# A hybrid attention and MoE layer on one core: where the transposes of x stand, and the scheme of the first q round

## Chip, core and metric

The kernel runs on one core of a Trainium2 chip. The metric is the device time of one execution in microseconds (us). Everything is float32. One core has the matrix engine PE (TensorE; its weight loads are listed apart as PEld), the vector engine DVE (VectorE), the activation engine ACT (ScalarE), POOL (GpSimd), and SP (SyncE), whose queue issues most DMAs. Each engine works through its instructions in order and waits on semaphores. PE writes to psum only, 8 banks of 512 float32 columns on 128 partitions.

## What is computed

One layer over 512 latent and 128 context tokens (640 rows of 1024). Cut to what bears on the change:

```python
mod = silu(c) @ w_ada + b_ada                 # 2 vectors (latent, context), 6 x 1024 columns each
shift1, scale1, gate1, shift2, scale2, gate2 = split(mod, 6)
h = rms_norm(x, norm1_g) * (1 + scale1) + shift1
z = h @ w_in                                  # cb, cc, cx, q, k, v, gc, ga
q = rms_norm(q.reshape(b, l, 8, 2, 64), q_norm_g)      # the same for k
if latent: q, k = axial_rope(q), axial_rope(k)
s = softmax(q k / sqrt(64)) of both halves;  a = p[0] - lam * p[1];  o = rms_norm(a @ v)
lam = exp(sum(lambda_q1 * lambda_k1)) - exp(sum(lambda_q2 * lambda_k2)) + lam_init
mixed = sigmoid(gc) * y_conv + sigmoid(ga) * (o @ w_attn_out)
x = x + gate1 * (mixed @ w_o)
x = x + gate2 * hier_moe(rms_norm(x, norm2_g) * (1 + scale2) + shift2)   # 16 experts, top 2 of a group
```

## The kernel before

The order of every engine's work is written out by hand; there is no planner. The stages are: load x and the first modulation weights; modulation and transposed h (`hT`, 8 blocks of 128 features by 640 tokens); for each of two groups of four heads a q round, a k round, a v round and attention; then feature products, the output projection, routing, and the 16 experts.

**Start.** The modulation is `silu(c) @ w_ada`, made in pairs of two 512-column pieces, pair p by the job `ada` p: 8 k-steps times 2 lanes, each a 64-row by 512-column matmul. In the records one float32 matmul is two, so a job has 32. The row result is copied from psum by ACT (`ada_copy`, L774), transposed by PE (job `adaT`, L1677), and DVE adds the bias and makes the scale (L1063, L1070). Pairs 0 and 1 are shift1 and scale1, half of the features each. Their weights stand in the four slots of `weight_ring` and come in two halves (`s_early`, then `s_w`). PE also transposes the normalized x (`xn`): the job `xT` k is feature block k, 5 transposes into two psum banks. ACT (odd k, L785) or DVE (even k, L1079) then writes `hT` block k as scale times psum plus shift, so it needs the modulation of that block's pair: pair 0 for k under 4, pair 1 for the others. With two banks each, only four jobs of the start fit in psum.

**Rounds.** A round makes q, k or v of one group of heads: 640 tokens by 512 columns. There are two schemes:

- plain: five tiles of 128 tokens (`tok_job`), each 8 matmuls of 512 columns; tile 0 (`i == 0`) stands apart in two halves of 64 tokens and has 16.
- seven products (`product_mm`): tile 0 is made plainly, and the other four tiles in two sets of seven products p1 to p7 (Strassen's scheme, 4 matmuls of 256 columns each), 14 products in all. It needs four sums of `hT` (`th`, by DVE, `token_sums`, held in the memory of x) and four sums of the weights (`round_sum`, by POOL, L622). DVE reads the products out and adds them up (`read_product`, L1151 and L1164), ACT copies p1 (`first_copy`). They leave rows in `v_sb`, `kept`.

Before the change the very first q round (m = 0) was plain, all other rounds used products. After each tile: ACT squares, DVE normalizes (`qk_stats`, `qk_norm`, L1120 to L1134), POOL does the rotary part (`rope`, L659 to L662), PE transposes (`qk_T`, L1750) and ACT copies to `qT` or `kT`. The rotary tables `ropeC` and `ropeS` and `lam` are made by DVE once, L1092 to L1110; the exponential for `lam` is on ACT (L810), ahead of its work on the first q tile.

**Banks.** The list JOBS gives each psum job a number and who empties it. In the rounds job j uses bank j mod 8, and PE opens a job only when the job that last used the bank was emptied. The core of it:

```python
def open_job(kind, n):
    for before in FREED_BY[INDEX[(kind, n)]]:
        emptied(pe, before)
```

Of the kernel before, what the change touches and what calls it, by code (L numbers as in the profile page):

```python
# [12 lines left out]
NT = T // P  # L13
# [51 lines left out]
def is_plain(z):  # L65

    return z < NT or z % NT == 0
# [47 lines left out]
def psum_jobs():  # L115

    def xT(k):
        return ("xT", k, "dve" if k % 2 == 0 else "act")

    def T(z):  # L120
        return [("qkT", z, "act")]

    def products(m, a, *inside):
        jobs = []
        for name in PRODUCTS:
            jobs.append(("prod", (m, a, name), "act" if name == "p1" else "dve"))
            for after, more in inside:
                if after == name:
                    jobs += more
        return jobs  # L130

    jobs = [("ada", 0, "act"), xT(1), ("adaT", 0, "dve"), xT(0), xT(3), ("ada", 1, "act"), xT(2), ("adaT", 1, "dve")]
    jobs += [xT(k) for k in (5, 4, 7, 6)]
    for g in range(GROUPS):
        z = round_start(g, Q)
        if g == 0:
            for zz in range(NT):
                jobs.append(("qk", zz, "dve"))
                if zz:
                    jobs += T(zz - 1)  # L140
            jobs.append(("ada", 2, "act"))
        else:
            jobs += [("qk", z, "dve")] + products(3, 0, ("p3", T(z))) + products(3, 1, ("p2", T(z + 1)))
        z = round_start(g, K)
        jobs.append(("qk", z, "dve"))
        if g == 0:
            jobs += T(z - 1) + [("adaT", 2, "dve")] + products(1, 0, ("p3", T(z))) + [("ada", 3, "act")]
            jobs += products(1, 1, ("p7", [("adaT", 3, "dve")]), ("p2", T(z + 1)))
        else:
            jobs += T(z - 3) + products(4, 0, ("p1", T(z - 2)), ("p5", T(z - 1)), ("p3", T(z)))  # L150
            jobs += products(4, 1, ("p2", T(z + 1)))
# [20 lines left out]
EMPTIED = []  # L172
_count = {"dve": 0, "act": 0}
for _, _, _who in JOBS:
    _count[_who] += 1
    EMPTIED.append((_who, _count[_who]))


def job_bank(j):

    if j < INDEX[("qk", 0)]:
        return 2 * (j % 4)
    if j < INDEX[("wo", 0)]:
        return (j - INDEX[("qk", 0)]) % 8
    return 2 * ((j - INDEX[("wo", 0)]) % 4)


def banks_of(j):

    return {job_bank(j), job_bank(j) + 1} if j < INDEX[("qk", 0)] else {job_bank(j)}  # L190
# [9 lines left out]
def build(nc, io):  # L200
# [4 lines left out]
    with ExitStack() as ctx:  # L205
# [235 lines left out]
        def kept_count(z):  # L441
            return 4 * (z // NT - 1) + z % NT
# [19 lines left out]
        def _(sp):  # L462
# [33 lines left out]
            job_done(sp, "qk", NT - 1)  # L496
# [102 lines left out]
        def _(pool):  # L599
# [24 lines left out]
            def round_sum(m, step):  # L624
                if step == 0:
                    pool.wait_ge(s_raw[m % 2], 16 * (m // 2 + 1))
                weight_sum(raw_slot[m % 2], sum_slot[m % 2], step, s_ws, 4 * (m - 1))

            def rope(z):
# [4 lines left out]
                if zz == 0:  # L634
                    if g == 0:
                        job_done(pool, "ada", 1)
                    else:
# [131 lines left out]
        def _(act):  # L769
# [68 lines left out]
            def first_copy(m, a):  # L838
                if (m, a) == (3, 0):
                    act.wait_ge(s_vread, 6)  # L840
                elif (m, a) != (1, 0):
                    emptied(act, INDEX[("prod", (m, 0, "p4") if a else (m - 1, 1, "p4"))])
                evict("prod", (m, a, "p1"), first_p, job_psum("prod", (m, a, "p1"))[:, 0:256])

            for g in range(GROUPS):
                z = round_start(g, Q)
                qk_stats(z)
                if g == 0:
                    for zz in range(1, NT):
                        qk_stats(zz)  # L850
                        qkT_copy(zz - 1)
                    ada_copy(2)
                else:
                    first_copy(3, 0)
                    qkT_copy(z)
                    qk_stats(z + 1)
                    first_copy(3, 1)
                    qk_stats(z + 2)
                    qkT_copy(z + 1)
                z = round_start(g, K)  # L860
                if g == 0:
                    qkT_copy(z - 1)
                    qk_stats(z)
                    first_copy(1, 0)
                else:
                    qk_stats(z - 2)
                    qk_stats(z - 1)
                    qkT_copy(z - 3)
                    qk_stats(z)
                    first_copy(4, 0)  # L870
                    qkT_copy(z - 2)
                    qkT_copy(z - 1)
# [163 lines left out]
        def _(dve):  # L1036
# [52 lines left out]

            dve.wait_ge(s_rows, 16)  # L1090
# [51 lines left out]
            def token_sums(sums_, src, step, made):  # L1142
                s11, s12, s21, s22 = (src[:, 4 * d:4 * d + 4, HALF * t:HALF * (t + 1)] for d in range(2) for t in range(2))
                if step:
                    dve.wait_ge(made, step)
                a_, b_ = ((s12, s11), (s22, sums_[:, 0]), (s22, s12), (s21, sums_[:, 1]))[step]
                V.tensor_tensor(sums_[:, step], a_, b_, sub).then_inc(made, 1)

# [32 lines left out]
            for g in range(GROUPS):  # L1181
                z = round_start(g, Q)
                if g == 0:
                    for zz in range(NT):
                        qk_norm(zz)
                        if zz < 4:
                            if zz == 0:
                                dve.wait_ge(s_xn, NT)
                                for k in (6, 7):
                                    emptied(dve, INDEX[("xT", k)])  # L1190
                            token_sums(th, hT, zz, s_th)
                else:
                    qk_norm(z)
                    products_start(3, 0)
                    products_end(3, 0)
                    qk_norm(z + 1)
                    products_start(3, 1)
                    qk_norm(z + 2)
                    products_end(3, 1)
                    qk_norm(z + 3)  # L1200
                    qk_norm(z + 4)
# [450 lines left out]
        def _(pe):  # L1652
# [27 lines left out]
            def early_ada(p):  # L1680
                ps = open_job("ada", p)
                srcs = [slot[2 * p + c].rearrange("p (k n) -> p k n", k=KT) for c in range(2)]
                pe.wait_ge(s_early[p], 32)
                ada_part(p, ps, range(0, 4), srcs)
# [68 lines left out]
            for g in range(GROUPS):  # L1753
                z = round_start(g, Q)
                if g == 0:
                    for zz in range(NT):
                        tok_job("qk", zz, 0, TIME[zz])
                        if zz:
                            qk_T(zz - 1)
                    ada(2)  # L1760
                else:
                    tok_job("qk", z, 3, 0)
# [8 lines left out]
                tok_job("qk", z, m, 0)  # L1771
                if g == 0:
                    qk_T(z - 1)
                    ada_T(2)
                    product(m, 0, "p1", "p6", "p7", "p5", "p2", "p3")
                else:
                    qk_T(z - 3)
                    product(m, 0, "p1")
                    qk_T(z - 2)
                    product(m, 0, "p6", "p7", "p5")  # L1780
                    qk_T(z - 1)
                    product(m, 0, "p2", "p3")
# [383 lines left out]
```

## Time and profile before

| | us |
|---|---|
| median of 3 runs | 1289.95 |
| lowest and highest | 1288.04, 1290.37 |
| the profiled execution, its own time | 1290.02 |
| its span (first to last instruction) | 1287.8 |
| PE busy in the span | 1238.4 (96%) |
| DVE, ACT, POOL busy | 596.3, 232.1, 346.8 |

PE is busy nearly throughout from 16 us on. So PE is read first, and the question in each stretch is what it does, at which granted clock, and what ends its idle times. Where a row of PE is followed by the next one, the distance of their starts is what a group costs; the duration of a group reaches a little over the start of the next, since matmuls are pipelined.

### The profile page before, as it was taken

How to read it: one execution, taken by the hardware profiler on the slowest of the kernel's cores; microseconds unless marked ns; L12 is line 12 of the kernel's file. 1: busy time of each engine (PE TensorE's matmuls, PEld its weight loads, DVE VectorE, ACT ScalarE, POOL GpSimd, SP SyncE). 2: the span in 40 equal slices, each digit the busy share in tenths (PEclk: the TensorE clock that was granted, in tenths of full speed). 3: DMA queues.
4: the chain of work that ended last, by engine and by line, in shares of the span. 5: the costliest groups of instructions: out<-in, count | busy, mean ns of one | idle time of the engine just before them, and what ended most of it. 6: DMA issues, size and time to landing. Idle time of an engine off the chain costs nothing.

```text
span 1287.8 us, 12590 instructions
## 1 busy us (share of the span) xinstructions
PE 1238.4 (96%) x4864; PEld 767.6 (60%) x4865; DVE 596.3 (46%) x1083; ACT 232.1 (18%) x483; POOL 346.8 (27%) x227
## 2 busy tenths in 40 slices
PE   4999998999999999999999999999989999999996
PEld 1446677776777767767777777555444444444442
DVE  2433378454776772673255354367421313222223
ACT  3211257123560002001100100111110101010100
POOL 0444400466002333333333330000311322222222
PEclk9999999999999999999999999999999999999998
DMA  9854120012201211221111154412898888889761
GB/s 353 285 187 163 51 74 1 17 66 74 75 1 47 85 49 40 88 83 68 66 66 66 66 211 165 147 66 94 317 422 352 353 341 341 351 322 363 299 245 33
DMA packets 59991, 209.04 MB, mean 162 GB/s; under 512 B 9568, under 2 KB 10144, under 8 KB 53792
## 3 DMA queue, kind: packets, MB, share of 16 engines
q1 hardware_dynamic: 47328, 186.25, 37.7%
q0 software_dynamic: 12000, 20.48, 4.5%
q10 hardware_dynamic: 608, 1.58, 0.3%
q8 instruction: 35, 0.57, 0.2%
q14 instruction: 20, 0.16, 0.0%
HBM read 208.24 MB, written 23.10 MB: 180 GB/s over the span
## 4 chain that ended last, share of the span: by engine, by line
PE 90%; DVE 4%; DMA 3%; issue 1%; ACT 1%; POOL 0%; SPq 0%; DVEq 0%; POOLq 0%
PE psum L1898 31%; PE psum L2055 16%; PE psum L1737 9%; PE psum L2074 8%; PE psum L1962 5%; PE psum L1831 3%; PE psum L1715 3%; PE psum L1665 3%; PE psum L1880 3%; DMA weight_ring<-in_w 2%; PE psum L1718 2%; DVE arena L1318 1%; PE psum L1862 1%; DMA weight_ring<-in_w_ada 1%; PE psum L2035 1%
## 5 line engine op out<-in xcount | busy, mean ns | idle before, releaser
L622 POOL TENSOR_TENSOR weight_ring<-weight_ring 128x1024 f32<-128x1024 f32 x76 | 185.2, 2445 | 333.2 <-DMA weight_ring<-in_w_in 176.3
L1898 PE MATMUL psum<-arena,weight_ring 128*128 128x320 f32 x928 | 256.9, 432 | 0.0
L2055 PE MATMUL psum<-weight_ring,arena 128*128 128x512 f32 x512 | 222.7, 592 | 2.3 <-DMA weight_ring<-in_w 1.7
L1898 PEld LDWEIGHTS psum<-arena,weight_ring 128*128 128x128 f32 x928 | 176.0, 190 | 72.6
L1898 PE MATMUL psum<-x,weight_ring 128*128 128x320 f32 x640 | 181.7, 436 | 2.3 <-DVE arena L1342 2.3
L2055 PEld LDWEIGHTS psum<-weight_ring,arena 128*128 128x128 f32 x512 | 96.1, 190 | 117.4 <-issue 116.5
L1898 PEld LDWEIGHTS psum<-x,weight_ring 128*128 128x128 f32 x640 | 121.9, 192 | 53.2 <-DVE arena L1342 3.5
L2074 PE MATMUL psum<-arena 128*128 128x512 f32 x256 | 112.6, 593 | 0.7 <-ACT arena L1003 0.7
L1607 DVE SCALAR_TENSOR_TENSOR arena<-psum,ropeC,arena 128x512 f32<-128x512 f32 x16 | 12.0, 751 | 193.1 <-ACT arena L999 193.1
L1342 DVE TENSOR_TENSOR arena<-psum,arena 128x320 f32<-128x320 f32 x124 | 59.4, 487 | 85.9 <-PE psum L1898 85.2
L2074 PEld LDWEIGHTS psum<-arena 128*128 128x128 f32 x256 | 47.5, 190 | 54.9 <-issue 54.0
L1737 PE MATMUL psum<-weight_ring,x 128*128 128x256 f32 x320 | 73.2, 380 | 0.0
L1962 PE MATMUL psum<-weight_ring,arena 128*128 128x512 f32 x160 | 71.7, 597 | 0.0
L1737 PEld LDWEIGHTS psum<-weight_ring,x 128*128 128x128 f32 x320 | 60.0, 190 | 8.8 <-issue 1.1
L1342 DVE TENSOR_TENSOR arena<-psum,ropeC 128x320 f32<-128x320 f32 x40 | 19.7, 491 | 93.4 <-PE psum L1898 93.3
L702 POOL DMA_INDIRECT y_sample<-arena,slot_rows_lat x16 | 30.8, 1925 | 114.1 <-DVE arena L1626 106.8
L963 ACT ACTIVATE ropeC<-psum 128x320 f32<-128x320 f32 x28 | 12.2, 437 | 268.3 <-PE psum L1898 229.5
L1737 PE MATMUL psum<-weight_ring,arena 128*128 128x256 f32 x240 | 56.1, 381 | 0.0
L696 POOL DMA_INDIRECT arena<-y_sample,slot_rows_lat x16 | 16.4, 1026 | 140.2 <-DMA y_prompt<-arena,slot_rows_ctx 132.6
L1267 DVE TENSOR_REDUCE softmax_stats<-psum 128x2 f32<-128x1280 f32 x32 | 47.5, 1488 | 13.2 <-PE psum L1831 12.7
L919 ACT ACTIVATE arena<-psum,softmax_stats 128x640 f32<-128x640 f32 x64 | 50.5, 791 | 12.4 <-DVE softmax_stats L1267 12.4
L1619 DVE TENSOR_TENSOR arena<-psum,arena 128x512 f32<-128x512 f32 x32 | 22.1, 691 | 64.8 <-PE psum L2074 64.8
(266 smaller groups left out, 1365.7 us busy)
## 6 DMA issues: line engine op xcount, KB each, us to landing
weight_ring<-in_w SPq DMA_DIRECT2D x32, 2048.0 KB, 13.0
weight_ring<-in_w_in SPq DMA_DIRECT2D x16, 2048.0 KB, 8.0
arena<-in_w SPq DMA_DIRECT2D x16, 2048.0 KB, 12.2
arena<-in_w_ada SPq DMA_DIRECT2D x6, 2048.0 KB, 12.9
weight_ring<-in_w_ada SPq DMA_DIRECT2D x8, 1024.0 KB, 14.4
x<-in_x_sample SPq DMA_DIRECT2D x2, 2048.0 KB, 12.4
weight_ring<-in_w_conv_out SPq DMA_DIRECT2D x2, 2048.0 KB, 7.7
weight_ring<-in_w_attn_out SPq DMA_DIRECT2D x2, 2048.0 KB, 7.7
```

What stands on the lines that cost most here:

```text
L622: nc.gpsimd.tensor_tensor(out, a_, b_, op).then_inc(signal, 1)
L919: last = A(prob[n % 2][:, c, :], S[:, KEYS * c:KEYS * (c + 1)], ACT.Exp, bias=st[:, c:c + 1], accum_out=st[:, 4 + c:5 + c])
L1267: V.reduce_max(sm[:, 8 * (n % 4):8 * (n % 4) + 2], S2, axis=AX, negate=True).then_inc(s_max, 1)
L1342: return V.tensor_tensor(out, product_psum(q, name), value, add)
L1665: last = mm(ps[LANE * lane:LANE * (lane + 1), 0:512], lanes_c[:, k, :], w[:, k, :], start=(k == 0), stop=(k == KT - 1))
L1715: last = mm(ps[LANE * half:LANE * (half + 1), 0:512], hT[:, k, HALF * half:HALF * half + LANE], w, start=(k == 0), stop=(k == KT - 1))
L1737: last = mm(ps[:, 0:256], x_[:, k, :], w_[:, k, :], start=(k == 0), stop=(k == 3))
L1831: last = mm(psum[:, base + KEYS * c + lo:base + KEYS * c + hi], q, kT[64 * c:64 * (c + 1), h, key:key + hi - lo], start=True, stop=True)
L1898: last = mm(product_psum(q, name), w[:, k, :], src[:, k, :], start=(k == 0), stop=(k == 3))
L1962: last = mm(ps[:, 0:512], mixT[:, k, P * i:P * (i + 1)], w[:, k, :], start=(k == 0), stop=(k == KT - 1))
L2055: last = mm(psum[:, 1024 + 512 * j:1536 + 512 * j], xgT[:, t, :], w[:, t, :], start=(t == 0), stop=(t == KT - 1))
L2074: last = mm(psum[:, 2560 + 512 * half:3072 + 512 * half], hhT[:, t, :], w[:, t, 512 * half:512 * (half + 1)], start=(t == 0), stop=(t == 3))
```

## The change

1. Start. Three transposes of x, `xT` 1, 0 and 3, stand between the two halves of `ada` 0. `xT` 2 stands ahead of `ada` 1, `xT` 5 and 4 between its halves, `xT` 7 and 6 around `adaT` 1. A table of banks (START_BANK) replaces the rule, and `ada` and `adaT` now take one bank each.
2. First q round in the seven-product scheme. POOL makes its weight sums ahead of the first rope (it waits for `ada` 1, whose weights hold the slots 2 and 3).
3. The h sums (`token_sums`) stand ahead of `lam` and the rotary tables on DVE; before, they stood one each behind the first four norms.
4. Products wait for the single sums that they read, not for all four.
5. In the k round of group 0 the transposes of the q tiles 2, 3 and 4 stand where group 1 had them; two of them were in the q round before.

```diff
-    jobs = [("ada", 0, "act"), xT(1), ("adaT", 0, "dve"), xT(0), xT(3), ("ada", 1, "act"), xT(2), ("adaT", 1, "dve")]
-    jobs += [xT(k) for k in (5, 4, 7, 6)]
+    jobs = [xT(1), xT(0), xT(3), ("ada", 0, "act"), ("adaT", 0, "dve"), xT(2), xT(5), xT(4), ("ada", 1, "act"), xT(7), ("adaT", 1, "dve"), xT(6)]
...
+START_BANK = {("xT", 1): 0, ("xT", 0): 2, ("xT", 3): 4, ("ada", 0): 6, ("adaT", 0): 7, ("xT", 2): 0, ("xT", 5): 2, ("xT", 4): 4, ("ada", 1): 6,
+              ("xT", 7): 0, ("adaT", 1): 7, ("xT", 6): 2}
...
-        return 2 * (j % 4)
+        return START_BANK[JOBS[j][:2]]
...
+            job_done(pool, "ada", 1)
+            for step in range(4):
+                round_sum(0, step)
...
+                            if part == 0 and m == 2:
+                                job_done(pool, "prod", (0, 1, "p4"))
...
+            dve.wait_ge(s_xn, NT)
+            for k in (6, 7):
+                emptied(dve, INDEX[("xT", k)])
+            for step in range(4):
+                token_sums(th, hT, step, s_th)
             dve.wait_ge(s_rows, 16)
...
-            early_ada(0)
+            early_ada(0, 0)
             x_T(1)
-            ada_T(0)
             x_T(0)
             x_T(3)
-            early_ada(1)
+            early_ada(0, 1)
+            ada_T(0)
             x_T(2)
+            early_ada(1, 0)
+            x_T(5)
+            x_T(4)
+            early_ada(1, 1)
+            x_T(7)
             ada_T(1)
-            for k in (5, 4, 7, 6):
-                x_T(k)
+            x_T(6)
...
-                pe.wait_ge(s_th, 4)
-                pe.wait_ge(s_ws, 4 * m)
                 for name in names:
+                    if name in ("p6", "p7", "p4"):
+                        pe.wait_ge(s_th, {"p6": 2, "p7": 3, "p4": 4}[name])
+                    if name in ("p6", "p7", "p5", "p3"):
+                        pe.wait_ge(s_ws, 4 * m + {"p6": 3, "p7": 2, "p5": 1, "p3": 4}[name])
...
+                tok_job("qk", z, 3 * g, 0)
                 if g == 0:
-                    for zz in range(NT):
-                        tok_job("qk", zz, 0, TIME[zz])
-                        if zz:
-                            qk_T(zz - 1)
+                    product(0, 0, *PRODUCTS)
+                    product(0, 1, "p1", "p6", "p7")
+                    qk_T(z)
+                    product(0, 1, "p5", "p2", "p3")
+                    qk_T(z + 1)
+                    product(0, 1, "p4")
                     ada(2)
```

What stands on PE in a row at the start, before: L1665 is `ada`, L1693 is `xT` (5 matmuls a job), L1677 is `adaT`, L1715 the first q tile.

```order
L1665 MATMUL psum<-weight_ring,slot_one_hots 64x512 x16
L1693 MATMUL psum<-ident,arena 128x128 x5
L1677 MATMUL psum<-ident,arena 128x128 x4
L1693 MATMUL psum<-ident,arena 128x128 x10
L1665 MATMUL psum<-weight_ring,slot_one_hots 64x512 x16
L1693 MATMUL psum<-ident,arena 128x128 x5
L1677 MATMUL psum<-ident,arena 128x128 x4
L1693 MATMUL psum<-ident,arena 128x128 x20
L1715 MATMUL psum<-weight_ring,arena 64x512 x16
```

The same of the changed kernel, where L1660 is `ada`, L1690 `xT`, L1672 `adaT` and L1717 the first q tile:

```order
L1660 MATMUL psum<-weight_ring,slot_one_hots 64x512 x8
L1690 MATMUL psum<-ident,arena 128x128 x15
L1660 MATMUL psum<-weight_ring,slot_one_hots 64x512 x8
L1672 MATMUL psum<-ident,arena 128x128 x4
L1690 MATMUL psum<-ident,arena 128x128 x5
L1660 MATMUL psum<-weight_ring,slot_one_hots 64x512 x8
L1690 MATMUL psum<-ident,arena 128x128 x10
L1660 MATMUL psum<-weight_ring,slot_one_hots 64x512 x8
L1690 MATMUL psum<-ident,arena 128x128 x5
L1672 MATMUL psum<-ident,arena 128x128 x4
L1690 MATMUL psum<-ident,arena 128x128 x5
L1717 MATMUL psum<-weight_ring,arena 64x512 x16
```

Between the end of `ada` 0 and the start of `ada` 1 there were three `xT` jobs and `adaT` 0; now there are `adaT` 0 and one `xT`.

PE in the first q round before, its last plain tile (L1718) with its transpose (L1750), then `ada` 2 and the k round's first tile:

```order
L1718 MATMUL psum<-weight_ring,arena 128x512 x8
L1750 MATMUL psum<-ident,arena 128x128 x4
L1665 MATMUL psum<-arena,slot_one_hots 64x512 x16
L1715 MATMUL psum<-weight_ring,arena 64x512 x16
L1750 MATMUL psum<-ident,arena 128x128 x4
```

And now, from the first q tile on; L1739 are products (those that read `x` use the h sums) and L1754 is the transpose:

```order
L1717 MATMUL psum<-weight_ring,arena 64x512 x16
L1739 MATMUL psum<-weight_ring,arena 128x256 x4
L1739 MATMUL psum<-weight_ring,x 128x256 x12
L1739 MATMUL psum<-weight_ring,arena 128x256 x8
L1739 MATMUL psum<-weight_ring,x 128x256 x4
L1739 MATMUL psum<-weight_ring,arena 128x256 x4
L1739 MATMUL psum<-weight_ring,x 128x256 x8
L1754 MATMUL psum<-ident,arena 128x128 x4
L1739 MATMUL psum<-weight_ring,x 128x256 x4
L1739 MATMUL psum<-weight_ring,arena 128x256 x8
L1754 MATMUL psum<-ident,arena 128x128 x4
L1739 MATMUL psum<-weight_ring,x 128x256 x4
```

Four plain tiles of 8 matmuls of 512 columns have become 14 products of 4 matmuls of 256 columns, and two transposes have left this stretch.

On DVE, behind its last copy of `hT` (L1079), stood the products of lambda and the tables:

```order
L1079 TENSOR_SCALAR arena<-psum,scale_g,mod 128x128
L1092 TENSOR_TENSOR arena<-rows 128x128
L1093 TENSOR_REDUCE neglam<-arena 128x2
L1096 TENSOR_SCALAR rows<-rows 128x64
L1101 TENSOR_TENSOR ropeC<-arena,rows 128x256
```

Now the four h sums (L1095) stand between:

```order
L1079 TENSOR_SCALAR arena<-psum,scale_g,mod 128x128
L1095 TENSOR_TENSOR x<-arena 128x1280
L1095 TENSOR_TENSOR x<-arena,x 128x1280
L1095 TENSOR_TENSOR x<-arena 128x1280
L1095 TENSOR_TENSOR x<-arena,x 128x1280
L1104 TENSOR_TENSOR arena<-rows 128x128
L1105 TENSOR_REDUCE neglam<-arena 128x2
```

## Rows read from the trace of the kernel before

**Rows 1.** The page: busy time of PE; granted clock of PE in 40 slices.
```profile
PE 1238.4 (96%) x4864; PEld 767.6 (60%) x4865; DVE 596.3 (46%) x1083; ACT 232.1 (18%) x483; POOL 346.8 (27%) x227
...
PEclk9999999999999999999999999999999999999998
```

**Rows 2.** Timeline of PE, 8 to 62 us: start, duration, line, [idle before <-releaser].
```profile
16.25 9.86 PE L1665 MATMUL psum<-weight_ring,slot_one_hots 128*64 128x512 f32 x32 [16.25 <-DMA weight_ring<-in_w_ada]
26.04 0.77 PE L1693 MATMUL psum<-ident,arena 128*128 128x128 f32 x5
...
29.14 7.09 PE L1665 MATMUL psum<-weight_ring,slot_one_hots 128*64 128x512 f32 x32 [0.60 <-ACT arena L785]
36.16 0.77 PE L1693 MATMUL psum<-ident,arena 128*128 128x128 f32 x5
...
37.48 2.35 PE L1693 MATMUL psum<-ident,arena 128*128 128x128 f32 x20
40.02 7.09 PE L1715 MATMUL psum<-weight_ring,arena 128*64 128x512 f32 x32 [0.19 <-issue]
47.03 7.13 PE L1718 MATMUL psum<-weight_ring,arena 128*128 128x512 f32 x16
55.05 0.63 PE L1750 MATMUL psum<-ident,arena 128*128 128x128 f32 x4 [0.88 <-POOL arena L662]
```

**Rows 3.** Line L1665 on PE, 17.2 to 18.2 us, then 23.2 to 24.2: ns min/median/max.
```profile
L1665 PE MATMUL psum<-weight_ring,slot_one_hots x6: 1061/1061/1113, 16.3 to 18.0; 128*64 128x512 f32 x6
...
L1665 PE MATMUL psum<-weight_ring,slot_one_hots x6: 592/592/592, 22.9 to 23.8; 128*64 128x512 f32 x6
```

**Rows 4.** Timelines of ACT, then DVE, between ada 0 and hT block 1.
```profile
26.14 0.60 ACT L774 ACTIVATE arena<-psum 128x512 f32<-128x512 f32 x1 [6.75 <-PE psum L1665]
27.96 2.14 ACT L785 ACTIVATE arena<-psum,mod,scale_g 128x512 f32<-128x512 f32 x4 [1.22 <-DVE scale_g L1070]
...
27.49 0.24 DVE L1063 TENSOR_TENSOR mod<-psum,cols 128x8 f32<-128x8 f32 x2 [9.91 <-PE psum L1677]
```

**Rows 5.** Timeline of PE, 56 to 160 us: ada 2 after the first q round; first k round.
```profile
77.79 7.09 PE L1665 MATMUL psum<-arena,slot_one_hots 128*64 128x512 f32 x32
...
92.61 1.89 PE L1737 MATMUL psum<-weight_ring,arena 128*128 128x256 f32 x8
...
102.97 0.60 PE L1750 MATMUL psum<-ident,arena 128*128 128x128 f32 x4
103.41 1.89 PE L1737 MATMUL psum<-weight_ring,x 128*128 128x256 f32 x8
...
125.41 7.09 PE L1715 MATMUL psum<-weight_ring,arena 128*64 128x512 f32 x32
```

**Rows 6.** Timelines of DVE and POOL; lines L1147 and L622: count, ns min/median/max.
```profile
50.95 2.02 DVE L1147 TENSOR_TENSOR x<-arena 128x1280 f32<-128x1280 f32 x1
...
50.47 1.16 POOL L659 TENSOR_TENSOR arena<-arena,ropeS 128x256 f32<-128x256 f32 x1 [12.57 <-DVEq L1137]
...
L1147 DVE TENSOR_TENSOR arena<-arena x8: 1479/1481/1483, 577.7 to 715.5; 128x1280 f32<-128x1280 f32 x8
...
L622 POOL TENSOR_TENSOR weight_ring<-weight_ring x10: 2348/2356/3595, 54.9 to 138.7; 128x1024 f32<-128x1024 f32 x10
```

**Rows 7.** Timeline of DVE: the first row of lambda and tables, the last of norm 0.
```profile
40.93 0.28 DVE L1092 TENSOR_TENSOR arena<-rows 128x128 f32<-128x128 f32 x1
...
50.35 0.69 DVE L1134 TENSOR_TENSOR arena<-arena,ropeC 128x512 f32<-128x512 f32 x1
```

**Rows 8.** PE timeline, feature stage; windows: PE, PEld, DVE, ACT, POOL busy, clock, DMA.
```profile
464.64 6.27 PE L1898 MATMUL psum<-x,weight_ring 128*128 128x320 f32 x16 [1.92 <-DVE arena L1342]
470.74 4.47 PE L1898 MATMUL psum<-arena,weight_ring 128*128 128x320 f32 x16
...
466.00:467.00 1.00, 1.00 (x3) 0.67 (x2) 0.97 (x4) 0.44 (x1) 0.00 (x0) 0.50 0.00 0
...
901.80:905.20 3.40, 3.40 (x10) 0.95 (x8) 2.71 (x10) 2.73 (x3) 1.36 (x1) 0.50 1.04 443
```

More of the change, by code:

```diff
@@ L65, in is_plain @@
 def is_plain(z):
-    return z < NT or z % NT == 0
+    return z % NT == 0
+START_BANK = {("xT", 1): 0, ("xT", 0): 2, ("xT", 3): 4, ("ada", 0): 6, ("adaT", 0): 7, ("xT", 2): 0, ("xT", 5): 2, ("xT", 4): 4, ("ada", 1): 6,
+              ("xT", 7): 0, ("adaT", 1): 7, ("xT", 6): 2}
+START_EMPTIED = [("ada", 0), ("adaT", 0), ("xT", 1), ("xT", 0), ("xT", 3), ("xT", 2), ("ada", 1), ("adaT", 1), ("xT", 5), ("xT", 4), ("xT", 7), ("xT", 6)]
 FEATURES = [("cc", 0), ("cx", 0), ("cb", 0), ("cc", 1), ("cx", 1), ("cb", 1), ("gc", 0), ("gc", 1), ("cv", 0), ("cv", 1), ("ga", 0), ("ga", 1),
@@ L171 @@
 INDEX = {(kind, n): j for j, (kind, n, _) in enumerate(JOBS)}
-EMPTIED = []
+EMPTIED = [None] * len(JOBS)
 _count = {"dve": 0, "act": 0}
-for _, _, _who in JOBS:
+for _j in [INDEX[name] for name in START_EMPTIED] + list(range(len(START_EMPTIED), len(JOBS))):
+    _who = JOBS[_j][2]
     _count[_who] += 1
-    EMPTIED.append((_who, _count[_who]))
+    EMPTIED[_j] = (_who, _count[_who])
 def job_bank(j):
     if j < INDEX[("qk", 0)]:
-        return 2 * (j % 4)
+        return START_BANK[JOBS[j][:2]]
     if j < INDEX[("wo", 0)]:
@@ L495, in _ @@
             load_pair(2)
-            job_done(sp, "qk", NT - 1)
+            job_done(sp, "prod", (0, 1, "p4"))
             load_round(0, V_ROUND)
@@ L634, in rope @@
                 if zz == 0:
-                    if g == 0:
-                        job_done(pool, "ada", 1)
-                    else:
+                    if g:
                         emptied(pool, INDEX[("kcT", g - 1)])
@@ L847, in _ @@
                 qk_stats(z)
-                if g == 0:
-                    for zz in range(1, NT):
-                        qk_stats(zz)
-                        qkT_copy(zz - 1)
-                    ada_copy(2)
[L853 to L872, printed above, removed]
+                first_copy(3 * g, 0)
+                if g:
+                    qkT_copy(z)
+                qk_stats(z + 1)
+                first_copy(3 * g, 1)
+                if g == 0:
+                    qkT_copy(z)
+                qk_stats(z + 2)
+                qkT_copy(z + 1)
+                z = round_start(g, K)
+                qk_stats(z - 2)
+                qk_stats(z - 1)
+                if g == 0:
+                    ada_copy(2)
+                qkT_copy(z - 3)
+                qk_stats(z)
+                first_copy(3 * g + 1, 0)
+                qkT_copy(z - 2)
+                qkT_copy(z - 1)
                 qkT_copy(z)
@@ L1088, in _, with token_sums @@
             xT_copy(6)
+            def token_sums(sums_, src, step, made):
+                s11, s12, s21, s22 = (src[:, 4 * d:4 * d + 4, HALF * t:HALF * (t + 1)] for d in range(2) for t in range(2))
+                if step:
+                    dve.wait_ge(made, step)
+                a_, b_ = ((s12, s11), (s22, sums_[:, 0]), (s22, s12), (s21, sums_[:, 1]))[step]
+                V.tensor_tensor(sums_[:, step], a_, b_, sub).then_inc(made, 1)
+            dve.wait_ge(s_xn, NT)
[3 more added lines that the diff above has]
+                token_sums(th, hT, step, s_th)
             dve.wait_ge(s_rows, 16)
@@ L1140, in _ @@
             rp = rowpack[:, :].rearrange("p (s v k) -> p s v k", s=4, v=2)
[L1142 to L1147, printed above, removed]
             def read_product(m, a, name, out, value):
@@ L1182, in _ @@
                 z = round_start(g, Q)
[L1183 to L1201, printed above, removed]
+                qk_norm(z)
+                products_start(3 * g, 0)
+                products_end(3 * g, 0)
+                qk_norm(z + 1)
+                products_start(3 * g, 1)
+                qk_norm(z + 2)
+                products_end(3 * g, 1)
+                qk_norm(z + 3)
+                qk_norm(z + 4)
                 z = round_start(g, K)
@@ L1678, in ada_T, with early_ada @@
                 last.then_inc(s_job, 1)
-            def early_ada(p):
+            def early_ada(p, half):
                 ps = open_job("ada", p)
                 srcs = [slot[2 * p + c].rearrange("p (k n) -> p k n", k=KT) for c in range(2)]
-                pe.wait_ge(s_early[p], 32)
-                ada_part(p, ps, range(0, 4), srcs)
+                if half == 0:
+                    pe.wait_ge(s_early[p], 32)
+                    ada_part(p, ps, range(0, 4), srcs)
+                    return
                 for c in range(2):
@@ L1771, in _ @@
                 tok_job("qk", z, m, 0)
+                qk_T(z - 3)
                 if g == 0:
-                    qk_T(z - 1)
                     ada_T(2)
[L1775 to L1782, printed above, removed]
+                product(m, 0, "p1")
+                qk_T(z - 2)
+                product(m, 0, "p6", "p7", "p5")
+                qk_T(z - 1)
+                product(m, 0, "p2", "p3")
                 qk_T(z)
```

33 lines of the change are left out of this document (15 added, 18 removed).

## The prediction, on record before the changed kernel ran

> **What bounds the kernel now.** I read the page first: PE is busy 96% of the span and is granted its full clock in nearly every slice [rows 1]. So a microsecond of PE work taken away or put in shows one for one, and other engines matter only where PE waits for them. Next comes the timeline of PE over the stretch that the change touches [rows 2, 5]. To be seen there: PE starts at 16.25 on a DMA, and from then until 125.41 it has only three short waits: 0.60 before `ada` 1, 0.19 before the first q tile, 0.88 before the first q transpose. The first `ada` takes 9.79 us (16.25 to 26.04), the second 7.02 (29.14 to 36.16). The reason is not a DMA wait inside it: its matmuls are recorded at 1061 ns at first and at 592 later [rows 3], which is the lower level of the clock (1.2 GHz) and then the upper (2.4), after an idle start.
>
> **Part 1, the start: costed at +3.7 us.** I walk it from the same rows. The second half of `ada` 0 is 16 records, half of 7.02, 3.5 us. So its first half ends at 26.04 - 3.5 = 22.5. The three transposes of x put there cost 0.6 each (four of them take 37.48 to 39.83, 2.35) and end at 24.3; the second half ends at 27.85 instead of 26.04. The transposes fill no hole, since there was none; they delay the chain of the modulation by 1.8. That chain is: copy by ACT at 26.14, `adaT`, DVE at 27.49, ACT at 27.96 writing `hT` 1 in 2 of 4 instructions of 2.14 together [rows 4]. It let PE start at 29.14. Before, PE had three `xT` and `adaT` in this time and waited 0.6. Now it waits for the copy (0.7), does `adaT` to 29.3, and its next instruction, `xT` 2, needs the bank of `xT` 1. That bank is emptied at 29.1 + 1.8 = 30.95. So PE idles 1.65 there, with `ada` 1 queued behind though its weights and its bank are ready.
> Then `xT` 2 (0.6), half of `ada` 1 (3.5), `xT` 5 and 4 (1.25), the other half (3.5): 39.8. `xT` 7 to 40.4, `adaT` 1 from 40.7 to 41.3. Last stands `xT` 6, in the bank of `xT` 5, and `xT` 5 can only be copied out with the modulation that `adaT` 1 has just made: DVE 0.5, ACT 1.1, so PE idles 1.7 and runs `xT` 6 from 43.0 to 43.6. The first q tile starts at 43.75; before at 40.02 [rows 2]. That is +3.7. Two idle times of about 1.7 are new and the work is the same.
>
> **Part 2, the first q round: costed at -5.5 us, with 0.9 given back.** Before: 40.02 to 84.8, end of `ada` 2 (it starts at 77.79 and takes 7.02) [rows 5], 44.8. After: first tile 7.0; 14 products, priced from the k round, which has the same 14: 92.61 to 125.41 is 32.8, less `ada` 3 (7.02) and three transposes of 0.44 (102.97 to 103.41), 24.5; two transposes 0.9; `ada` 2 7.0. Sum 39.4, so -5.4 to -5.5. In it are the 0.88 wait (its rope now has ten microseconds of products as cover) and 3.6 of matmul work and of starts of groups. The two transposes that have moved to the k round cost 0.9 there. No weight of any round is loaded later than PE needs it: the v weights are released after the last product, at some 76 us, against 77 before.
>
> **What hides the new work of DVE and POOL.** The weight sums take 2.35 each on POOL, 4 of them 9.4; they can start at the end of `ada` 1, 39.9. The h sums take 1.48 each alone [rows 6] and start at 44.9, when `xT` 6 is copied. PE reaches p6 at 43.75 + 7.0 + 1.75 = 52.5 and needs the second h sum and the third weight sum there. But the two engines stop one another: the h sum that met a rotary multiplication took 2.02 instead of 1.48, and the longest weight sum 3.6 instead of 2.35 [rows 6]. Taken in turns (POOL to 47.1, DVE to 48.5, POOL to 50.8, DVE to 52.2) they are ready 0.3 before PE. If DVE ran all four first, the third weight sum would end at 53.2: PE would wait 0.7. I take 0 and keep 0.7 as the bound.
> The Trainium skill has a rule for this, "SBUF — State Buffer", section "Who interferes with whom": an operation of VectorE with two inputs in SBUF and one of GpSimd that reads SBUF exclude each other for whole instructions. The trace agrees (2.02 against 1.48). By it the wait is anything from 0 to 0.7; if they ran side by side it would be 0, so that the rule bears on the chance of the last rival alone.
> Behind the sums stand lambda and the tables on DVE, from 40.93 on before, and norm 0, whose last row starts at 50.35 and takes 0.69 [rows 7]. Now lambda starts at 55, and ACT cannot square the first tile until the exponential is done. With the busy parts of that chain as they were (lambda and tables some 2.7, the norm some 3 behind them), norm 0 ends near 60.7, 10 us later than before. Who waits for that? The product readouts, and through the banks PE: the 8th product needs the bank of the first tile, read out at 60.1, and PE comes to it at 62.9. So 2.8 us of cover are left and nothing is paid. The first rope ends at 63.7, its transpose stands at 68.1.
>
> **The sum without the clock.** +3.7 - 5.5 + 0.9 = -0.9 us: 1290.0 (the profiled execution, which equals the median of 1289.95) goes to 1289.1.
>
> **Part 3, the clock.** This is where I chose. PE's clock is granted by what it did. A wait of 1.92 us in the feature stage, PE being full before it, was followed by a stretch at 0.50 (the 1.2 GHz level), in which 16 matmuls took 6.27 instead of 4.47, a loss of 1.8. A stretch from 901.8 to 905.2, after small matmuls and short waits, is at 0.50 as well [rows 8]. No wait under 1 us among full matmuls shows it, nor does the stretch from 36.16 to 40.02 that is transposes alone [rows 2]. The two new idle times are 1.65 (with 0.7 close before it and only four transposes between) and 1.7 (with transposes on both sides). Both are nearer to the 1.92 row than to the 0.9 ones. So I take it that the clock falls at one or at both of them in the median execution. One fall costs 1.5 to 1.8; below 1.8 where part of the low stretch is idle anyway. The bounds are 0 and 3.6; I take 2.4, between one and two.
>
> **Forecast: 1289.1 + 2.4 = 1291.5 us**, from 1290.6 (one fall) to 1292.4 (two of 1.65).
>
> **Rivals.**
> (a) The clock holds: 1289.1. For it: both gaps are shorter than 1.92, and the times before scatter by 2.3 us with the same program, so whether the clock falls somewhere is partly chance. Against: the first hole is 2.35 of idle time in 3 us. Chance 0.22.
> (b) Slower. Both falls at the full price, 3.6, give 1292.7; a low stretch that lasts as long again because the second hole falls into it (the one near 902 is a whole row of 3.4 us at 0.50) costs 1.7 more, 1294.4. It decides from 3.4 us of loss on. For it: `ada` 1 stands in small pieces between transposes. Against: those pieces are full matmuls of 3.5 us each. Chance 0.22.
> (c) Faster. The three transposes inside `ada` 0 are free after all, because its second half is in truth bound by the arrival of the second half of the weights, and the first hole shrinks with it: -1.8, so 1287.3 at a clock that holds. Against: the records of that job follow each other without an idle time, and their durations explain its length. Chance 0.09.
> (d) The sums come late, PE waits at p6 by up to 0.7, or the readouts eat up their 2.8 us of cover by one or two: 1291 to 1293. Chance 0.07, mostly no change.
> The forecast has 0.40.
>
> **How the numbers follow.** A measurement of this kernel can tell about 0.2%, 2.6 us, from no change: below 1287.4 is faster, above 1292.5 slower. Faster: (c), 0.09. Slower: (b) and a fourth of (d), with some of the forecast's upper end, 0.27. Within: 0.64. The range leaves out most of (c) and what lies beyond (b): 1288.3 to 1294.4.
>
> **What would show it.** PE: `ada` 0 ends near 27.9; idle of about 1.65 before the fourth `xT`, released by ACT, and of 1.7 before the last `xT`, released by ACT; the first q tile starts at 43.75 with the clock held, 45 to 47 without. A granted clock of 0.50 for a stretch after 31 or 43. Then 14 products in 24.5 without a wait, `ada` 2 starting 32.4 (7.0 + 24.5 + 0.9) behind the first tile's start. DVE's first norm near 58 to 61. It is wrong if the second half of `ada` 0 is seen to wait for a DMA, if the two idle times are under 1 us, or if a product waits for DVE or POOL by more than 1 us.

## The result

The changed kernel takes 1291.97 us in the median of 16 executions (1289.92 to 1294.13), the kernel before 1289.57 in the median of 16 (1287.78 to 1292.90). The ratio is 1.0015, with a 95% interval from 1.0009 to 1.0022: slower by 1.9 us (1.2 to 2.8), which is less than the 0.2% taken above as the bound of no change. The two medians lie 2.4 apart; the comparisons with the kernel before go by the ratio. The forecast was 1291.5, in a range from 1288.3 to 1294.4.

The profiled execution took 1294.13 us, at the upper end of the scatter; its span is 1292.4. First the page's rows that answer to [rows 1], busy time and granted clock:

```profile
PE 1239.6 (96%) x4912; PEld 776.8 (60%) x4913; DVE 605.3 (47%) x1097; ACT 233.2 (18%) x485; POOL 351.7 (27%) x231
...
PEclk9999999999999999999999999999899999999998
```

PE's busy time has not fallen by the matmul work that the products save, and its share is the same. Most of the reason is in the timeline of PE at the start, which answers to [rows 2] (start, duration, line, idle before it and who released it):

```profile
16.31 6.30 PE L1660 MATMUL psum<-weight_ring,slot_one_hots 128*64 128x512 f32 x16 [16.31 <-DMA weight_ring<-in_w_ada]
22.54 1.86 PE L1690 MATMUL psum<-ident,arena 128*128 128x128 f32 x15
24.33 3.65 PE L1660 MATMUL psum<-weight_ring,slot_one_hots 128*64 128x512 f32 x16
28.68 0.66 PE L1672 MATMUL psum<-ident,arena 128*128 128x128 f32 x4 [0.70 <-ACT arena L780]
31.03 0.77 PE L1690 MATMUL psum<-ident,arena 128*128 128x128 f32 x5 [1.69 <-ACT arena L791]
31.72 5.35 PE L1660 MATMUL psum<-weight_ring,slot_one_hots 128*64 128x512 f32 x16
37.00 1.31 PE L1690 MATMUL psum<-ident,arena 128*128 128x128 f32 x10
38.24 3.65 PE L1660 MATMUL psum<-weight_ring,slot_one_hots 128*64 128x512 f32 x16
41.83 0.77 PE L1690 MATMUL psum<-ident,arena 128*128 128x128 f32 x5
42.69 0.63 PE L1672 MATMUL psum<-ident,arena 128*128 128x128 f32 x4
45.58 1.33 PE L1690 MATMUL psum<-ident,arena 128*128 128x128 f32 x5 [2.26 <-ACT arena L791]
46.84 8.13 PE L1717 MATMUL psum<-weight_ring,arena 128*64 128x512 f32 x32
54.90 1.99 PE L1739 MATMUL psum<-weight_ring,arena 128*128 128x256 f32 x8
```

The reader is to see three things. No idle time stands before the second half of `ada` 0 at 24.33: it followed the transposes at once, so its weights were there. There are two idle times in front of a transpose of x, 1.69 and 2.26 us, both ended by ACT's copy of `hT` (L791). And directly behind each hole the same work is slower: half of `ada` 1 takes 5.35 and its other half 3.65; the first q tile takes 8.13, where the same tile took 7.09 before [rows 2].

The granted clock says why. Windows of one microsecond, columns as in [rows 8], the clock is the third number from the end:

```profile
32.00:33.00 1.00, 1.00 (x4) 0.24 (x2) 0.96 (x2) 0.00 (x0) 0.00 (x0) 0.50 1.26 240
33.00:34.00 1.00, 1.00 (x4) 0.24 (x2) 0.00 (x0) 0.00 (x0) 0.00 (x0) 0.50 1.18 244
...
46.00:47.00 1.00, 1.00 (x7) 0.67 (x7) 0.06 (x1) 0.98 (x3) 0.92 (x2) 0.50 0.00 0
47.00:48.00 1.00, 1.00 (x4) 0.36 (x6) 1.00 (x2) 0.84 (x1) 1.00 (x1) 0.50 0.02 6
```

0.50 is the lower level, 1.2 GHz. Each of the two stretches lasted 3.4 us. They cost 1.7 in `ada` 1 (5.35 less 3.65) and 1.6 in the last transpose and the q tile (1.33 less 0.77, and 8.13 less 7.09).

The q round itself, which answers to [rows 5]: its products begin at 54.90, and `ada` 2 stands behind them.

```profile
72.27 0.60 PE L1754 MATMUL psum<-ident,arena 128*128 128x128 f32 x4
...
78.33 1.89 PE L1739 MATMUL psum<-weight_ring,x 128*128 128x256 f32 x8
80.15 7.09 PE L1660 MATMUL psum<-arena,slot_one_hots 128*64 128x512 f32 x32
...
156.77 0.60 PE L1811 MATMUL psum<-ident,arena 128*128 128x128 f32 x4
```

From the end of the first tile to `ada` 2 it is 80.15 - 54.90 = 25.25, against 77.79 - 47.03 = 30.76 before: -5.5, and no row of PE in it has an idle time.

Behind the rounds the clock acts at two more places, and the prediction priced neither. In the feature stage, where the kernel before waited 1.92 us and then ran 16 matmuls in 6.27 [rows 8], the changed kernel (first line) waits 1.56 and the clock holds. That the shorter wait is not the whole reason is seen in e2 (second line), which waits 1.92 as before and holds its clock too:

```profile
467.47 4.57 PE L1901 MATMUL psum<-x,weight_ring 128*128 128x320 f32 x16 [1.56 <-DVE arena L1337]
...
471.44 4.57 PE L1910 MATMUL psum<-x,weight_ring 128*128 128x320 f32 x16 [1.92 <-DVE arena L1347]
```

The changed kernel is 3.2 us behind the kernel before at the end of the k round, and 1.1 behind after this row (the next group starts at 471.88 against 470.74). In the routing stage it comes to be 4.2 behind (918.96 against 914.76, the first row of L2045 and of L2042): the granted clock over 898 to 920 us is 0.77 there and was 0.84.

### The profile page after: what moved, and what is told of

Read it like the earlier page. It is cut to its first block, busy times and chain, and to the rows that moved or that the text cites. A ratio compares the mean times of both kernels' runs of the same rounds, so it can differ in the third digit from the quotient of the medians.

```text
span 1292.4 us, 12745 instructions
## 1 busy us (share of the span) xinstructions
PE 1239.6 (96%) x4912; PEld 776.8 (60%) x4913; DVE 605.3 (47%) x1097; ACT 233.2 (18%) x485; POOL 351.7 (27%) x231
## 4 chain that ended last, share of the span: by engine, by line
PE 93%; DVE 2%; DMA 2%; ACT 1%; issue 1%; POOL 0%; SPq 0%; ACTq 0%; DVEq 0%; POOLq 0%
PE psum L1901 32%; PE psum L2058 17%; PE psum L1739 11%; PE psum L2077 9%; PE psum L1965 5%; PE psum L1660 4%; PE psum L1834 3%; PE psum L1717 3%; PE psum L1883 3%; PE psum L1865 1%; DMA weight_ring<-in_w_ada 1%; PE psum L2038 1%; PE psum L1754 1%; PE psum L1871 1%; PE psum L2065 1%
## 5 line engine op out<-in xcount | busy, mean ns | idle before, releaser
L625 POOL TENSOR_TENSOR weight_ring<-weight_ring 128x1024 f32<-128x1024 f32 x80 | 194.3, 2437 | 370.8 <-DMA weight_ring<-in_w_in 130.9
L2058 PEld LDWEIGHTS psum<-weight_ring,arena 128*128 128x128 f32 x512 | 96.7, 192 | 116.7 <-issue 115.8
L1739 PE MATMUL psum<-weight_ring,x 128*128 128x256 f32 x384 | 87.8, 380 | 0.0
L1739 PEld LDWEIGHTS psum<-weight_ring,x 128*128 128x128 f32 x384 | 71.9, 190 | 10.3 <-issue 1.1
L1739 PE MATMUL psum<-weight_ring,arena 128*128 128x256 f32 x288 | 67.2, 381 | 0.0
L1739 PEld LDWEIGHTS psum<-weight_ring,arena 128*128 128x128 f32 x288 | 53.4, 190 | 10.9 <-issue 4.3
```

The costliest lines, as they stand in the source:

```text
L625: nc.gpsimd.tensor_tensor(out, a_, b_, op).then_inc(signal, 1)
L1739: last = mm(ps[:, 0:256], x_[:, k, :], w_[:, k, :], start=(k == 0), stop=(k == 3))
L2058: last = mm(psum[:, 1024 + 512 * j:1536 + 512 * j], xgT[:, t, :], w[:, t, :], start=(t == 0), stop=(t == KT - 1))
```

## Experiments

The executions of one kernel scatter by 3 to 7 us, so a comparison of medians is good to 1 or 2 us with five to twelve executions. The waits and the clock are read from the one profile of each kernel, with the time beside it. All times "against before" are ratios of runs on the same chip, times 1290.

**e1: the start of the kernel before, the product round kept.**

```diff
-            early_ada(0, 0)
-            x_T(1)
-            x_T(0)
-            x_T(3)
-            early_ada(0, 1)
-            ada_T(0)
-            x_T(2)
-            early_ada(1, 0)
-            x_T(5)
-            x_T(4)
-            early_ada(1, 1)
-            x_T(7)
-            ada_T(1)
-            x_T(6)
+            early_ada(0, 0)
+            early_ada(0, 1)
+            x_T(1)
+            ada_T(0)
+            x_T(0)
+            x_T(3)
+            early_ada(1, 0)
+            early_ada(1, 1)
+            x_T(2)
+            ada_T(1)
+            for k in (5, 4, 7, 6):
+                x_T(k)
```

(The list of jobs and the table of banks are changed with it; they are left out here.)

> The changed kernel with the start of the kernel before (order and banks of the transposes of x undone), the seven-product q round kept. Theory (the two idle times of the new start and the falls of the clock behind them cost the change its gain): against the kernel before -5.5 for the round and +0.9 for the two transposes moved, with up to 0.5 for a wait of p6 for the sums, which start 4 us nearer to it: -4.6 to -4.1 us, about 6.5 below the changed kernel; no stretch at 0.50 of the granted clock before 450 us. Rival (the product round itself gains little, because DVE comes late and PE waits in it): within 1.5 us of the kernel before, and waits of PE on DVE or POOL between 45 and 90 us.

Measured: 1284.88 us in the median of 5 (1283.23 to 1286.69), ratio 0.9963 (0.9948 to 0.9977), so -4.8 us. This is the fastest kernel here, faster than the kernel before and than the changed one. Its PE rows:

```profile
29.33 7.24 PE L1661 MATMUL psum<-weight_ring,slot_one_hots 128*64 128x512 f32 x32 [0.60 <-ACT arena L792]
...
40.38 7.09 PE L1716 MATMUL psum<-weight_ring,arena 128*64 128x512 f32 x32 [0.22 <-issue]
47.40 1.99 PE L1738 MATMUL psum<-weight_ring,arena 128*128 128x256 f32 x8
50.00 5.42 PE L1738 MATMUL psum<-weight_ring,x 128*128 128x256 f32 x24 [0.60 <-issue]
```

The q tile starts at 40.38 and `ada` 1 takes 7.24 in one piece; p6 starts at 50.00, after 0.60 of idle time. The row names no releaser; the second h sum was done at 47.7, and POOL's third weight sum ran from 46.42 to 49.90, so it is the weight sum that p6 waited for. `ada` 2 starts at 73.49 in this trace, 77.79 before and 80.15 with the change. The granted clock is 1.00 from 16 to 60 us (below) and from 60 to 160:

```profile
16.00:60.00 44.00, 41.93 (x198) 23.57 (x199) 24.59 (x36) 12.76 (x20) 14.56 (x7) 1.00 0.98 352
```

So the product round is worth about the 4.6 that the sum gave it (the interval is 3.0 to 6.7), and the rival that PE would wait in it falls.

**e2: the new start alone, with the plain q round.** The mirror of e1: the kernel before, with the jobs, the banks and PE's order of the changed one.

> The kernel before with the new start alone, the q round plain and the h sums where they were. Theory: +3.7 us of idle and order, and +3.0 for a fall of the clock at each of the two holes: +6.7 us against the kernel before, with two stretches at 0.50. Rival (the falls of the clock are chance and would come at this rate without the holes, or belong to the product round): +3.7 us in the median and no or one such stretch. With no weight sums on POOL at the second hole, that hole is 1.7 us and not the 2.26 of the changed kernel.

Measured: 1295.73 us in the median of 6 (1294.84 to 1299.73), ratio 1.0056 (1.0040 to 1.0072), +7.2 us against an expected 6.7 and, without the clock, 3.7.

```profile
30.55 0.96 PE L1700 MATMUL psum<-ident,arena 128*128 128x128 f32 x5 [1.69 <-ACT arena L790]
31.44 5.10 PE L1670 MATMUL psum<-weight_ring,slot_one_hots 128*64 128x512 f32 x16
...
44.48 1.22 PE L1700 MATMUL psum<-ident,arena 128*128 128x128 f32 x5 [1.69 <-ACT arena L790]
45.63 8.27 PE L1727 MATMUL psum<-weight_ring,arena 128*64 128x512 f32 x32
53.83 7.13 PE L1730 MATMUL psum<-weight_ring,arena 128*128 128x512 f32 x16
```

Both holes are 1.69, and behind each the work is slow. The second tile starts at 53.83 against 47.03 [rows 2], +6.8, which is the measured time nearly whole. The rival, +3.7 in the median and at most one fall, is out. e1 and e2 add up: -4.8 + 7.2 = 2.4, against the change's 1.9; with the 0.6 by which the second hole is longer in the changed kernel it is 3.0, so the sum closes to about 1 us and no better.

**e3: the holes filled.** Two matmuls with no use in each hole.

```diff
+            def fill(n):
+                for _ in range(n):
+                    mm(psum[:, 512 * START_BANK[("ada", 0)]:512 * START_BANK[("ada", 0)] + 448], ident[:, :], xn[:, 0, 0:448], start=True, stop=True)
...
             ada_T(0)
+            fill(2)
             x_T(2)
...
             ada_T(1)
+            fill(2)
             x_T(6)
```

> The changed kernel with two matmuls of 448 columns in each of the two idle times of the start, into a bank that is free there; their result is overwritten and no work is left out. They end about when the awaited copy does, so the idle times stay lost. Theory (clock): the two stretches at 0.50 are gone before 60 us, which in the profiled execution cost 1.75 in ada 1 and 1.7 in the last transpose and the first q tile: 3.0 to 3.5 us below the changed kernel, 0.5 to 1.2 below the kernel before. Rival (the low level costs nothing that the waits would not cost anyway): equal to the changed kernel, +2 against the kernel before.

Measured: 1290.57 us in the median of 11, ratio 1.0001 (0.9990 to 1.0012). A twelfth execution took 2657.83 us; why is not known, and it is left out. That is neither: 1.4 below the changed kernel (1.8 by the ratios), not 3. The profiled execution (1287.97 us) shows what the theory wanted, half of `ada` 1 at 3.65 and the q tile at 7.09, but also a hole that is not filled:

```profile
41.10 1.67 PE L1695 MATMUL psum<-arena,ident 128*128 128x448 f32 x4
44.20 0.77 PE L1690 MATMUL psum<-ident,arena 128*128 128x128 f32 x5 [1.43 <-ACT arena L791]
45.22 7.09 PE L1723 MATMUL psum<-weight_ring,arena 128*64 128x512 f32 x32 [0.25 <-ACT arena L791]
```

The wait at the second hole was longer than I had reckoned: POOL's first weight sum began at 40.62, and DVE's scale instruction in the awaited chain, which starts at 41.58, takes 1.41 us (0.74 in the changed kernel). The clock held in this profile although 1.43 was left idle. The eleven executions ran from 1286.65 to 1292.61, with a mean granted clock of 0.993 and 0.994 in the fastest three and of 0.991 in four of the five slowest; where in those it was low is not recorded. So the run was inconclusive, and e6 follows it up.

**e4: the first hole taken away by order.**

```diff
+            early_ada(1, 0)
             x_T(2)
-            early_ada(1, 0)
```

> The changed kernel with the first half of ada 1 ahead of xT 2 instead of behind it, one line moved, so that PE has 3.5 us of ready matmuls where it waited 1.69 for the bank of xT 1. Theory: -1.7 for the wait and -1.7 for the first fall of the clock, the second hole and fall stay: 3.4 us below the changed kernel, near -1.2 against the kernel before, one stretch at 0.50 left before 60 us. Rival (only the wait counts): 1.7 below the changed kernel. Rival (the copies are what bounds, the wait moves to the second hole): equal to the changed kernel, with a second hole of 3.9.

Measured: 1287.06 us in the median of 11 (1285.99 to 1288.74), ratio 0.9978 (0.9970 to 0.9987), -2.8 us; the expected -1.2 was too small. Against the changed kernel's 1.9 that is 4.7 less for one line moved.

```profile
29.07 3.65 PE L1660 MATMUL psum<-weight_ring,slot_one_hots 128*64 128x512 f32 x16
32.65 1.86 PE L1690 MATMUL psum<-ident,arena 128*128 128x128 f32 x15
34.44 3.65 PE L1660 MATMUL psum<-weight_ring,slot_one_hots 128*64 128x512 f32 x16
...
41.21 0.76 PE L1690 MATMUL psum<-ident,arena 128*128 128x128 f32 x5 [1.70 <-ACT arena L791]
42.22 8.58 PE L1717 MATMUL psum<-weight_ring,arena 128*64 128x512 f32 x32 [0.25 <-ACT arena L791]
```

The first hole and its slow stretch are gone, the second hole is 1.70 and the fall behind it is there (8.58). Its start sits at 42.22, which is 4.62 before the 46.84 of the changed kernel: 1.69 of wait, 1.7 of clock, 0.56 because the second hole is 1.70 here and 2.26 there, and 0.6 that the last transpose took less (0.76 against 1.33), less small change. I had counted only the first two. The last is no gain: the fall lands on the q tile instead (8.58 against 8.13), and at `ada` 2 the lead is 4.17 (75.98 against 80.15). The second hole is shorter because POOL's first weight sum, which also waits for the DMA of its weights, starts at 40.86, behind DVE's scale instruction (39.82, 0.17 us), and does not hold it up. Both rivals are out: 1.7 below the changed kernel, and a second hole of 3.9.

**e5: the changed kernel again, and e6: the second hole filled with four matmuls instead of two.**

> The changed kernel once more, as the measure for the other runs of this call. Both theories: +1.9 us against the kernel before (ratio 1.0015), executions between 1289.9 and 1294.1.

> The changed kernel with two matmuls in the first hole and four in the second, whose idle time was still 1.43 us with two of them (its wait is longer because POOL's weight sums hold up DVE there). Theory (the clock falls where idle time is left; in the timed executions with two and two it fell at the second hole in about half of them): no execution above 1291, median 3 us below the changed kernel of this call, 1288.5 to 1289.5. Rival (the scatter of the kernel with two and two comes from elsewhere, routing and the end, and filling buys 1.3 us at most): median 1290 to 1291 and a scatter as wide as before. No work is left out; what the added matmuls write is overwritten.

Measured: e5 1291.49 us in the median of 12 (1289.63 to 1293.11), ratio 1.0011 (1.0001 to 1.0020), which confirms the first result. e6 1288.82 in the median of 12 (1287.33 to 1293.92), ratio 0.9997 (0.9985 to 1.0008). The medians lie 2.7 apart (the ratios 1.8) with the idle times for the copies still paid; eight of the twelve executions of e6 lie at or below 1289.05 and four above 1290.4, one of them at 1293.92, against the "no execution above 1291" that I had put down. The clock over the same window of e5 and then of e6, each from its own profile:

```profile
28.00:60.00 32.00, 27.75 (x124) 14.01 (x125) 17.84 (x30) 8.40 (x15) 11.78 (x6) 0.89 0.95 333
```

```profile
28.00:60.00 32.00, 30.98 (x144) 16.54 (x145) 19.56 (x32) 9.09 (x16) 11.79 (x6) 1.00 0.95 336
```

0.89 over 32 us is 7 us at half clock, two stretches. With matmuls that do nothing useful in the holes it is 1.00, and the kernel is faster for it. That the holes take the clock down is shown by this and by e4; what makes the four slower executions of e6 was not traced.

The 2.7 is not the price of the two falls alone. In the profiles e6 is 1.7 ahead at the end of the k round (154.35 against 156.01). The two falls cost e5 3.0 there, and e6 gives 0.8 of it back, because DVE's scale instruction starts 0.8 us after a weight sum of POOL (40.85) and 1.6 after it in e5 (43.09 and 41.46), so that it waits longer for the end of the sum and takes 1.55 us in place of 0.74:

```profile
41.68 1.55 DVE L1070 SCALAR_TENSOR_TENSOR scale_g<-mod,cols 128x8 f32<-128x8 f32 x1
```

Later the lead is 4.3 behind the routing stage (granted clock over 898 to 920 us 0.84 in e6, 0.77 in e5) and 2.6 over the whole span.

**e7: the h sums behind lambda and the tables, on top of e1.** This undoes the third part of the change.

> The old start and the product round, as in the best run so far, with the h sums behind lambda and the rotary tables (the third part of the change undone). Theory: the h sums start 2.6 us later, and p6 waits for the second of them: 0.6 us of wait in e1_old_start becomes 2 to 3, over p6 and p7, and the time goes up by as much. Rival (the weight sums on POOL are what is late, they run ahead without the lock while DVE makes the tables): p6 waits 0.5 or less, and the time is that of e1_old_start.

One execution: 1291.99 us, 7 above the median of e1. PE waits 5.25, more than the 2 to 3 expected:

```profile
54.61 7.66 PE L1738 MATMUL psum<-weight_ring,x 128*128 128x256 f32 x24 [5.25 <-DVE x L1096]
```

and this is DVE before it (timeline, durations second):

```profile
41.28 1.63 DVE L1100 TENSOR_TENSOR arena<-rows 128x128 f32<-128x128 f32 x1
...
43.14 2.02 DVE L1104 TENSOR_SCALAR rows<-rows 128x64 f32<-128x64 f32 x1
45.20 2.62 DVE L1109 TENSOR_TENSOR ropeC<-arena,rows 128x256 f32<-128x256 f32 x1
...
51.54 1.49 DVE L1096 TENSOR_TENSOR x<-arena 128x1280 f32<-128x1280 f32 x1
```

The table instructions are tiny (0.28 and 0.18 us for the first and the 64-column one in the trace before, where POOL was idle), but here they and the next two become 1.3 to 2.2 us longer each: they wait for the rest of a weight sum of POOL, 2.35 us alone. The last table rows, behind POOL's last sum, are as short as before (0.41 and 0.48). The tables took 10 us instead of 2.6. So the theory had the direction, and the size came from a lock that I had reckoned with for the h sums and not for the tables. The wait took the clock down too: the three products behind it last 7.66 instead of 5.4. By this one execution, the product round without the third part of the change gains nothing over the kernel before (1290.06 in the median here).

**e8: POOL's first weight sums wait for `xT` 6, on top of the changed kernel.**

> The changed kernel with POOL's first weight sums waiting for xT 6 instead of ada 1. Theory (these sums lengthened the second hole by holding up DVE's scale instruction, 0.74 us instead of 0.17): the second hole is 1.7 us instead of 2.26. The sums then start near 45 instead of 42 and, taken in turns with the h sums, end near 60: p6 and p7 wait 1 to 2.5 us in all, so that nothing is won. Rival (the hole has another cause): the second hole stays at 2.2.

One execution: 1292.32 us, within the scatter of the changed kernel. The second hole is 1.69 in it, and DVE's scale instruction takes 0.17; in the changed kernel these were 2.26 and 0.74:

```profile
43.80 0.17 DVE L1070 SCALAR_TENSOR_TENSOR scale_g<-mod,cols 128x8 f32<-128x8 f32 x1
...
45.19 0.77 PE L1690 MATMUL psum<-ident,arena 128*128 128x128 f32 x5 [1.69 <-ACT arena L791]
46.20 8.58 PE L1717 MATMUL psum<-weight_ring,arena 128*64 128x512 f32 x32 [0.25 <-ACT arena L791]
54.72 1.99 PE L1739 MATMUL psum<-weight_ring,arena 128*128 128x256 f32 x8
56.55 5.34 PE L1739 MATMUL psum<-weight_ring,x 128*128 128x256 f32 x24
```

With e2, which has no weight sums there and a hole of 1.69 too, the cause of the longer hole is settled, and the rival falls. The wait of p6 and p7 that I expected did not come, though the weight sums started at 46.04 and ended at 59.0. The fall of the clock stayed.

## Why the prediction was right

- **What bounds** (PE, one for one): right up to the end of the rounds. `ada` 2 stands 2.4 us later in the trace (80.15 against 77.79), the last row of the k round 3.2 later (156.77 against 153.54), the 0.9 of the moved transposes with it. Behind them it is not one for one: the distance goes to 1.1 in the feature stage and to 4.2 in routing, each time with the granted clock.
- **Part 1, the start, +3.7:** right in its mechanism and nearly in size. `ada` 0 ended at 27.9 as worked out, the first hole is 1.69 (forecast 1.65). The second is 2.26 (1.7), because a weight sum of POOL held up the DVE scale instruction in the awaited chain; e8 shows it, and e2, with no weight sums there, has 1.69. I had weighed the lock between DVE and POOL only at p6.
- **Part 2, the q round, -5.5 + 0.9:** right. -5.5 in the trace, and e1 measured -4.8 where the sum gives -4.6, with the wait of 0.60 at p6 inside it. Its trace has -3.4 of that by the end of the k round (150.11 against 153.54).
- **Cover of the sums and the norm:** no product waited in the changed kernel. It is thinner than it looks: e1 pays 0.60, e7 5.25.
- **Part 3, the clock, +2.4:** the step on which sign and size hung. The choice that the clock falls was right, and the size was too small: the traces have both falls, 3.3 in the changed kernel (1.7 and 1.6) and 3.0 in e5, where 2.4 was taken. So the start and the rounds cost 3.2 in the trace where the forecast has 1.5. That the measured 1.9 lies so near to it is partly luck. In e5, whose profiled execution (1291.22) is near the median, the distance to the kernel before is 2.5 at the end of the k round, 0.4 behind the wait of the feature stage, 3.4 behind routing and 1.6 at the end, and the prediction priced none of what comes after the k round.
- **The rivals:** (a), that the clock holds, is contradicted by both profiles of the changed kernel, though how often it held in the other executions is not recorded. (c), a late second half of the weights, is refuted by the row at 24.33, which has no idle time. (d) did not occur. (b) has two parts: both falls at nearly the full price are what the traces show, and the longer stretch was not seen in the start. Its sum, 1292.7, is 0.7 above the measured median, which is less than what the later stages move, so the time does not decide between it and the forecast; the traces of the start stand nearer to (b). The profiled execution does lie at 1294.13, its span 4.6 above that of the kernel before, and in it the clock is also low for a stretch (0.72 over 942 to 948 us) that is at 1.00 before and in e5.

Not tried: a start that keeps the transposes inside `ada` 0 and fills both holes with useful work. e4 does it for one; the old order (e1) has a wait of only 0.60 to begin with.

## What to carry to other kernels

Before putting work into an assumed wait, find the wait as a row: here the long first `ada` was slow matmuls after an idle start and no wait for weights, so that the transposes put there only delayed the chain behind it. Then price an idle time of 1.7 us on PE with transposes around it at about twice its length, since the clock can fall behind it, and look for a line to move up (e4: one line, 4.7 us). When two edits come in one change, run them apart: -4.8 and +7.2 were hidden in a result of +1.9.

## What the hardware did that I had not expected

Idle times of 1.69 to 2.27 us on PE, between transposes in the start, were followed by 3.4 us at half clock all nine times in five profiles: at both places in the changed kernel, e5, e2 and e8, at the second in e4. The shortest such case known from the trace before was 1.92. That one is not certain: in the feature stage the same wait of 1.92 or 1.93 was followed by the low level in the kernel before, e1, e4, e7 and e8, and by the full clock in e2, e3 and e6, with the same groups of matmuls around it. So the length of a wait alone does not tell whether the clock falls; what else decides was not found here. And the lock between DVE and POOL is felt most by the smallest instructions: 0.28 us became 1.63, 0.17 became 0.74, because each waits for the rest of a 2.35 us sum, while two long streams just take turns (h sums of 3.52 in e1, 1.49 alone). The Trainium skill, "SBUF — State Buffer", section "Who interferes with whom", says that the second to issue blocks fully; the trace of e7 agrees: 10 us of tables instead of 2.6.
